# A hybrid decoder layer on one core: x transposed before it is normalised, the norm factors applied behind the first projection, last products and results tile by tile

## The reference

```
h  = RMSNorm(x) * g1
q_a,k_a,v_a | q_b,k_b,v_b | gate_a | gate_b = split(h @ W_in)      # 1024 x 4352
x += (sigmoid(gate_a) * (A @ W_a) + sigmoid(gate_b) * (B @ W_b)) @ W_o   # A, B: two attentions
x += CrossAttn(RMSNorm(x), RMSNorm(mem))                           # 256 memory tokens
x += HierMoE(RMSNorm(x))       # top-1 of 4 groups, top-2 of 8 experts, 32 gated MLPs of 256
out = RMSNorm(x) * g_final
RMSNorm(x) = x * (mean(x*x) + 1e-6) ** -0.5, row by row
```

## Time and profile before

| | us |
|---|---|
| median of 3 runs (lowest, highest) | 463.2 (462.82, 464.59) |
| the profiled execution's own time | 462.48 |
| its span, first to last instruction | 460.7 |
| PE busy | 405.1 |
| DVE busy | 176.8 |
| ACT busy | 166.3 |
| POOL busy | 38.9 |

### The profile page before, as it was taken

The page is one execution under the profiler, slowest core; times in us unless marked ns, Lnnn a source line. Parts: engine busy times, 40 slices in busy tenths (PEclk is TensorE's granted clock), DMA queues, the critical chain, the costliest instruction groups (busy, mean ns, idle before and its releaser), DMA issues.

```text
span 460.7 us, 7793 instructions
## 1 busy us (share of the span) xinstructions
PE 405.1 (88%) x3113; PEld 302.7 (66%) x3113; DVE 176.8 (38%) x314; ACT 166.3 (36%) x320; POOL 38.9 (8%) x81
## 2 busy tenths in 40 slices
PE   3999999999999999999999898989895758768476
PEld 3999998999999999999895343434251322413223
DVE  3663754766458846546444111111201101002003
ACT  6744657576468544567535000000100001001004
POOL 4010242223000000000302000000000000000000
PEclk9999999999999999999998999999999988979979
DMA  8878874767745855558989999999999999999992
GB/s 297 219 203 271 269 246 157 229 198 232 256 138 175 282 185 183 177 166 285 363 265 358 345 413 410 409 410 406 409 410 410 409 410 409 410 410 410 410 379 91
DMA packets 66228, 139.53 MB, mean 303 GB/s; under 512 B 6646, under 2 KB 40470, under 8 KB 66198
## 3 DMA queue, kind: packets, MB, share of 16 engines
q1 hardware_dynamic: 66192, 139.12, 82.7%
q10 hardware_dynamic: 6, 0.00, 0.0%
HBM read 138.06 MB, written 1.05 MB: 302 GB/s over the span
## 4 chain that ended last, share of the span: by engine, by line
PE 71%; DMA 11%; SPq 10%; DVE 2%; ACT 2%; issue 2%; POOLq 0%; POOL 0%; DVEq 0%; ACTq 0%
PE proj L1186 13%; PE proj L1187 13%; PE proj L1188 13%; DMA moe_slot<-in_expert_w_up_dram 10%; PE proj L1431 9%; SPq L365 5%; PE score L1455 4%; PE score L1405 3%; SPq L370 3%; SPq L364 3%; PE attno L1463 2%; PE attno L1261 1%; PE probt L1187 1%; PE probt L1188 1%; PE probt L1186 1%
## 5 line engine op out<-in xcount | busy, mean ns | idle before, releaser
L823 DVE TENSOR_TENSOR w_lo<-w_raw,w_hi 128x1024 fp32r<-128x1024 f32 x66 | 81.2, 1231 | 45.0 <-ACT w_hi L568 44.6
L1431 PE MATMUL proj<-moe_slot,moe_x 128*32 128x512 f32 x512 | 66.8, 668 | 30.2 <-DMA moe_slot<-in_expert_w_up_dram 22.5
L568 ACT ACTIVATE w_hi<-w_raw 128x1024 fp32r<-128x1024 f32 x66 | 69.8, 1059 | 30.5 <-PE proj L1188 21.8
L1186 PE MATMUL proj<-hT_hi,w_hi 128*128 128x256 f32 x232 | 67.2, 290 | 0.0
L1187 PE MATMUL proj<-hT_lo,w_hi 128*128 128x256 f32 x232 | 65.6, 283 | 0.0
L1188 PE MATMUL proj<-hT_hi,w_lo 128*128 128x256 f32 x232 | 65.6, 283 | 0.0
L1431 PEld LDWEIGHTS proj<-moe_slot,moe_x 128*32 128x32 f32 x512 | 17.7, 120 | 67.6 <-issue 56.1
L777 ACT ACTIVATE silu_g<-proj 128x256 f32<-128x256 f32 x8 | 3.1, 383 | 152.1 <-PE proj L1431 152.1
L1186 PEld LDWEIGHTS proj<-hT_hi,w_hi 128*128 128x128 f32 x232 | 44.4, 191 | 3.2 <-issue 2.0
L1187 PEld LDWEIGHTS proj<-hT_lo,w_hi 128*128 128x128 f32 x232 | 44.4, 192 | 0.0
L1188 PEld LDWEIGHTS proj<-hT_hi,w_lo 128*128 128x128 f32 x232 | 44.4, 191 | 0.0
(11 more groups left out here) (266 smaller groups left out, 755.1 us busy)
## 6 DMA issues: line engine op xcount, KB each, us to landing
moe_slot<-in_expert_w_gate_dram SPq DMA_DIRECT2D x64, 512.0 KB, 14.6
moe_slot<-in_expert_w_up_dram SPq DMA_DIRECT2D x64, 512.0 KB, 15.2
moe_slot<-in_expert_w_down_dram SPq DMA_DIRECT2D x64, 512.0 KB, 14.7
w_raw<-in_w_in_dram SPq DMA_DIRECT2D x34, 512.0 KB, 4.4
w_raw<-in_xattn_wkv_dram SPq DMA_DIRECT2D x8, 512.0 KB, 3.5
w_raw<-in_mix_out_w_dram SPq DMA_DIRECT2D x8, 512.0 KB, 3.5
w_raw<-in_moba_out_w_dram SPq DMA_DIRECT2D x4, 512.0 KB, 3.9
w_raw<-in_swa_out_w_dram SPq DMA_DIRECT2D x4, 512.0 KB, 3.5
```

What stands on the lines that cost most here:

```text
L568: act.activation(w_hi[:, g % NS], w_raw[:, g % NW], ACT.Copy).then_inc(hi_done, 1)
L823: dve.tensor_tensor(w_lo[:, g % NS], w_raw[:, g % NW], w_hi[:, g % NS].bitcast(F32), ALU.subtract)\
L1186: pe.matmul(ps, a[0], b[0], start=start, stop=False, skip_group_check=True)
L1431: op = pe.matmul(PJ[0][e * WIN:(e + 1) * WIN, :].rearrange("p (j f) -> p j f", j=2), moe_x[:, k, e * WIN:(e + 1) * WIN], both_w[:, r], sta ...
```

## The change

- The tiles of x are transposed as they land. Their squares are still summed and the factors still computed, but no engine needs them before a result of the first projection is copied out.
- The copies of chunks 0 to 16 multiply by the factors. For qa, ka, qb, kvb and the gates the token runs along the free axis, so the factors are needed as a row on all partitions (`rnorm_row`): PE makes it by two products, DVE copies it. These copies move from ACT to DVE. For va the token is the partition; ACT keeps that copy, now one for each tile.
- SP's queue begins with the first norm's weights, then tile 0, weight half 0, tile 1, halves 1 and 2. The other three norm weights are loaded from ACT's queue.
- The small products for sinks and biases, and the transpose of the three other norm weights, move behind the third weight half (g == 2), together with the two products for `rnorm_row`.
- At the end products and squares go tile by tile, POOL adds epsilon itself, and ACT issues one of the four stores.

```diff
-    ON_DVE = {"merge": 1, "mix": 1, "xo": 2}
+    ON_DVE = {"qa": 1, "ka": 1, "qb": 1, "kvb": 1, "gate": 1, "merge": 1, "mix": 1, "xo": 2}
@@ SP
-            for t in range(TT):
-                sp.dma_start(xres[:, t], x[0, t * P:(t + 1) * P, :]).then_inc(x_in[t], 16)
-            for i, g in enumerate((mix_norm_g, mem_norm_g, xattn_norm_g, ffn_norm_g)):
-                sp.dma_start(g_rows[i * KD:(i + 1) * KD, :], g[0].rearrange("(k p) -> k p", p=P)).then_inc(gain_in, 16)
-            for g in range(NW):
+            sp.dma_start(g_first[:], mix_norm_g[0].rearrange("(k p) -> k p", p=P)).then_inc(first_gain_in, 16)
+            sp.dma_start(xres[:, 0], x[0, 0:P, :]).then_inc(x_in[0], 16)
+            load_half(0)
+            sp.dma_start(xres[:, 1], x[0, P:T, :]).then_inc(x_in[1], 16)
+            for g in range(1, NW):
                 load_half(g)
...
-            for t in range(TT):
-                for half, scaled in ((1, fin_dve), (0, fin_act)):
-                    cols = slice(half * 512, (half + 1) * 512)
-                    sp.wait_ge(scaled, t + 1)
-                    sp.dma_start(out[0, t * P:(t + 1) * P, cols], fin_rows[:, t, cols]).then_inc(out_done, 16)
+            for t, half in ((0, 1), (0, 0), (1, 1)):
+                cols = slice(half * 512, (half + 1) * 512)
+                sp.wait_ge(fin_dve if half else fin_act, t + 1)
+                sp.dma_start(out[0, t * P:(t + 1) * P, cols], fin_rows[:, t, cols]).then_inc(out_done, 16)
@@ POOL
-            inverse_root(4)
+            for t in range(TT):
+                pool.wait_ge(sq_done, sq_count(FINAL_NORM, t))
+                pool.tensor_scalar(mean_eps[:, FINAL_NORM, t:t + 1], mean_sq[:, FINAL_NORM, t, 0:1],
+                                   mean_sq[:, FINAL_NORM, t, 1:2], EPS, ALU.add, ALU.add).then_inc(ms_done, 1)
+                pool.wait_ge(ms_done, 2 * FINAL_NORM + t + 1)
+                pool.tensor_tensor(rnorm[:, FINAL_NORM, t:t + 1], mean_eps[:, FINAL_NORM, t:t + 1], mhalf[:, 0:1],
+                                   ALU.pow).then_inc(rs_done, 1)
@@ ACT
+            for i, g in enumerate((mem_norm_g, xattn_norm_g, ffn_norm_g)):
+                act.dma_start(g_rows[i * KD:(i + 1) * KD, :], g[0].rearrange("(k p) -> k p", p=P)).then_inc(gain_in, 16)
...
-            for t in range(TT):
-                act.wait_ge(x_in[t], 16)
-                whole_squares(0, xres, t)
-            act.wait_ge(rs_done, 1)
-            act.activation(xn[:, 0], xres[:, 0], ACT.Copy, scale=rnorm[:, 0, 0:1]).then_inc(x0n_done, 1)
+            act.wait_ge(x_in[0], 16)
+            whole_squares(0, xres, 0)
             split_hi(0)
...
             unit_hi(0, hT_hi, 3)
+            act.wait_ge(x_in[1], 16)
+            whole_squares(0, xres, 1)
             for c in range(FIRST_UNDER):
                 split_hi(2 * c + 2)
                 split_hi(2 * c + 3)
-                evacuate(c)
+                if kinds[c] not in ON_DVE:
+                    evacuate(c)
...
+            act.wait_ge(fin_act, TT)
+            act.dma_start(out[0, P:T, 0:512], fin_rows[:, 1, 0:512]).then_inc(out_done, 16)
@@ DVE
+            def evacuate(c):
+                k, i, src = kinds[c], kinds[:c].count(kinds[c]), PJ[c % 2]
+                two = src[:].rearrange("p (a n) -> p a n", a=2)
+                rows = rnorm_row[:].unsqueeze(1).broadcast_to([P, 2, T])
+                dve.wait_ge(half_done, 2 * c + 2)
+                if k in ("qa", "qb"):
+                    op = dve.scalar_tensor_tensor(out=(qa if k == "qa" else qb)[:, 2 * i:2 * i + 2], in0=two,
+                                                  scalar=float(HD) ** -0.5, in1=rows, op0=ALU.mult, op1=ALU.mult)
...
+                else:
+                    op = dve.tensor_tensor(gates[:, 2 * i:2 * i + 2], two, rows, ALU.mult)
+                op.then_inc(ev_dve, 1)
...
-            normalise(0, xres, [1])
...
+            for t in range(TT):
+                means(0, t)
             for c in range(FIRST_UNDER):
                 split_lo(2 * c + 2)
                 split_lo(2 * c + 3)
+                if c == 0:
+                    dve.wait_ge(row_ps, 1)
+                    dve.tensor_copy(rnorm_row[:], PO[1][:, T:2 * T]).then_inc(row_set, 1)
...
+                    dve.wait_ge(row_set, 1)
+                if kinds[c] in ON_DVE:
+                    evacuate(c)
                 if c == 1:
                     normalise(MEM_NORM, mem_raw)
...
                 split_lo(2 * c + 3)
+                evacuate(c)
                 if 2 <= i <= UNITS + 1:
                     mix_out_lo(i - 2)
@@ PE
-            pe.transpose(PO[0][:, 0:4 * KD], g_rows[:], ident[0:4 * KD, 0:4 * KD]).then_inc(c_gain_ps, 1)
-            transpose_normalised(((x0n_done, 1), (xn_done, 1)))
+            pe.transpose(PO[0][:, 0:KD], g_first[:], ident[0:KD, 0:KD]).then_inc(c_gain_ps, 1)
+            for t in range(TT):
+                pe.wait_ge(x_in[t], 16)
+                for u in range(4):
+                    op = transpose_unit(NT_BANKS, xres, u, t)
+                    if t == TT - 1:
+                        op.then_inc(nt_ps, 1)
...
+                if g == 2:
+                    consts = PO[0][:, P:]
...
+                    pe.wait_ge(rs_done, TT)
+                    for t in range(TT):
+                        op = pe.matmul(PO[1][:, T + t * P:T + (t + 1) * P],
+                                       rnorm[:, 0, t:t + 1].broadcast_to([P, P]), ident[:], start=True, stop=True)
+                    op.then_inc(row_ps, 1)
...
                     back_to_tokens(0, 0)
-                    back_to_tokens(1, 0)
                     pe.wait_ge(y_dve, n + 1)
-                    for t in range(TT):
-                        back_to_tokens(t, 1)
+                    back_to_tokens(0, 1)
+                    for half in range(2):
+                        back_to_tokens(1, half)
```

More of the change, by code:

```diff
@@ L480, in _ @@
             inverse_root(0)
[L481 removed]
+            pool.wait_ge(c_gain, 2)
             pool.wait_ge(wr_in, 32)
@@ L663, in _ @@
             split_hi(2 * at["merge"] + 2)
-            act.wait_ge(ev_act, evac_count(last["gate"]))
+            act.wait_ge(ev_dve, evac_count(last["gate"]))
             sigmoids(0)
@@ L866, in mix_out_lo @@
                     .then_inc(mix_lo, 1)
-            normalise(0, xres, [1])
+            def evacuate(c):
[6 more added lines that the diff above has]
+                                                  scalar=float(HD) ** -0.5, in1=rows, op0=ALU.mult, op1=ALU.mult)
+                elif k == "ka":
+                    op = dve.tensor_tensor(ka[:, 2 * i:2 * i + 2], two, rows, ALU.mult)
+                elif k == "kvb":
+                    for g in range(2):
+                        for half in range(2):
+                            dve.tensor_tensor(kb2[half * HD:(half + 1) * HD, g], src[g * HD:(g + 1) * HD, 0:T],
+                                              rnorm_row[g * HD:(g + 1) * HD], ALU.mult)
+                    for t in range(TT):
+                        op = dve.tensor_scalar(vb[:, t], src[:, T + t * P:T + (t + 1) * P], rnorm[:, 0, t:t + 1], None,
+                                               ALU.mult)
+                else:
+                    op = dve.tensor_tensor(gates[:, 2 * i:2 * i + 2], two, rows, ALU.mult)
+                op.then_inc(ev_dve, 1)
             dve.wait_ge(c_gain_ps, 1)
-            dve.tensor_copy(gains[:], PO[0][:, 0:4 * KD].rearrange("p (n k) -> p n k", n=4)).then_inc(c_gain, 1)
+            dve.tensor_copy(gains[:, 0], PO[0][:, 0:KD]).then_inc(c_gain, 1)
             split_lo(0)
@@ L1226, in pair_scores @@
                 swa, i = divmod(j, PAIRS)
-                pe.wait_ge(ev_act, evac_count(at["kvb"] if swa else at["ka"] + i // 2))
+                pe.wait_ge(ev_dve, evac_count(at["kvb"] if swa else at["ka"] + i // 2))
                 if j:
@@ L1252, in pair_values @@
                 swa, i = divmod(j, PAIRS)
-                pe.wait_ge(ev_act, evac_count(at["kvb"] if swa else at["va"] + i // 2))
+                if swa:
+                    pe.wait_ge(ev_dve, evac_count(at["kvb"]))
+                else:
+                    pe.wait_ge(ev_act, evac_count(at["va"] + i // 2))
                 pe.wait_ge(pt_sb, 2 * j + 2)
@@ L1279, in _ @@
                     half_chunk(g, hT_hi, hT_lo)
-            pe.wait_ge(c_gain, 3)
+                if g == 2:
+                    consts = PO[0][:, P:]
+                    pe.wait_ge(c_gain, 1)
+                    pe.wait_ge(gain_in, 48)
+                    pe.transpose(consts[:, 0:3 * KD], g_rows[:], ident[0:3 * KD, 0:3 * KD])
+                    consts = consts[:, 3 * KD:]
+                    pe.wait_ge(c_ones, 1)
+                    pe.wait_ge(small_in, 48)
+                    pe.matmul(consts[:, 0:HEADS], ones[0:1, :], sink_row[:], start=True, stop=True)
+                    pe.matmul(consts[:, HEADS:HEADS + NG + NE], ones[0:1, :], br[:], start=True, stop=True)
+                    pe.wait_ge(rs_done, TT)
```

(5 more changed lines are left out.)

92 lines of the change are left out of this document (38 added, 54 removed).

## The result

The changed kernel took 466.2 us (median of 20 runs, 464.6 to 467.6) against 463.3 for the kernel before on the same chip: a ratio of 1.0056, with a 95% interval from 1.004 to 1.0073. The ratios of this document compare means, so they are not the quotients of the medians beside them, and two executions of the kernel before, of 1022 and 2219 us, are left out of this one. Forecast were 462.8 us and a range up to 464.8, so both the time and the sign of the change were missed. The profiled execution of the changed kernel took 464.86 us of its own, with a span of 463.0; the kernel before, 462.48 and 460.7. These 2.4 us can be followed through the two traces. In the table a row is a place in the program, in us from the start of the span; the first four are starts in PE's timelines.

A forecast was written before the change was run, and what follows sets the result against it. PE's pace was taken to bound the kernel until 133 us and the start of the later expert-load stream; -1.8 + 0.75 + 0.15 + 1.5 - 0.45 = +0.15 on 462.48 gave 462.6, forecast 462.8 us, range 460.9 to 464.8 (8 in 10).

The forecast's parts named there:

- tile 1 at 7.4: At the start, tile 1 of x lands at 7.4 us behind weight half 0; bounds 6.7 and 8.5.
- the clock term: At the start, TensorE's clock rises late because PE's transposes are broken up by gaps: +1.5 us, bounds 0 and 2.5.
- the step from the profile to the median: Sum on the profiled execution gave 462.6; only part of its 0.7 below the median was added, giving 462.8 us.
- First product, -1.8: At the start, PE's first projection product comes at 9.9 instead of 11.7 us: -1.8, bounds -2.5 and -0.7.
- The cross-check in the prediction: At the start, the queue carries the same bytes up to tile 1 as it did before up to 7.36 us.
- lands at 8.5, first product at 11: Rival at the start: tile 1 lands late behind a weight half, clock as late, 463.9 us; chance 0.15.
- Constants, +0.75: Between weight halves 2 and 3, PE does small products, norm-weight transpose and `rnorm_row` products: +0.75 us, bounds 0.5 and 1.1.
- DVE behind `rnorm_row`, +0.15: At `w_lo` of half 4, DVE's way of 2.9 us stalls PE: +0.15 us, bounds 0 and 1.2.
- The rival of a DVE stall of 1.5 us: Rival around `rnorm_row`: DVE's way takes 4 us, costing 1.5 in all, 464.3 us; chance 0.13.
- Copies on DVE, 0: In projections and attention, copies moved from ACT to DVE cost nothing, up to +1 if one delays a `w_lo`.
- The end, -0.45: At the end, the last two stores go out together and the last lands near 459.9: -0.45 us, bounds -0.9 and 0.
- the 0.05 above 465.5: Chance of a measurably slower kernel, above 465.5 us: late landing of tile 1 and DVE's stall together, 0.05.

The follow-up runs named there:

- e14: e10 with the first norm's weights issued behind tile 1 of x instead of first; 465.3 us, ratio 1.004.
- e13: e10 with weight half 1 and all loads behind it held until tile 0 has landed; 462.5 us, ratio 0.9968.
- e1: Changed kernel with PE's gaps before the first product filled by identity transposes that nobody reads (12, 9 and 5); 462.5 us, ratio 0.999.
- e8: The changed kernel run once more, unaltered; 465.9 us, ratio 1.0044.
- e2: Changed kernel with tile 1 of x loaded ahead of weight half 0; 466.5 us, ratio 1.0073.
- e5: e1 with the norm-weight transpose and the products for sinks and biases moved between the two tiles; 462.4 us, ratio 0.9977.
- e7: Kernel before with 28 filling transposes at the start and the changed kernel's new end; 461.4 us, ratio 0.9963.
- e3: Kernel before with 28 filling identity transposes ahead of its first transpose; 461.6 us, ratio 0.9967.
- `A`: The changed kernel, against the kernel before; 466.2 us, ratio 1.0056.
- `B`: The kernel before the change, base of the ratios; 463.3 us.
- e11: e7 with the experts' norm weights and both router-weight loads issued behind weight half 3; 461.15 us, ratio 0.9954.
- e12: Changed kernel with only the 12 filling transposes at the start, none behind the tiles; 465.7 us, ratio 1.0052.
- e9: The kernel before once more, unaltered, for its trace; profiled own time 462.34 us.
- e4: Kernel before with only the changed kernel's new end; 463.8 us, ratio 1.0001.
- e6: e1 with the three other norm weights loaded from SP's queue behind weight half 2, not ACT's; 462.3 us, ratio 0.998.
- e10: e5 with the experts' norm weights and both router-weight loads issued behind weight half 3; 462.3 us, ratio 0.998.

## Why the prediction was wrong

Against the profile's own times the forecast sum was +0.15 and the traces say +2.4. Three steps failed: "tile 1 at 7.4", the size of the clock term, and the step from the profile to the median. By the terms:

- **First product, -1.8: was -0.5.** The step that failed is "tile 1 at 7.4". It landed at 8.4 in the profile, and between 8.38 and 8.79 in the five profiles with the same loads. The cross-check in the prediction (the queue carries the same bytes up to 7.36 as before) left out its own first line, the 0.45 us of the issue ahead (e14: 0.5 on tile 0, 0.34 on tile 1), and took transfers to be served one behind the other; when the two halves right behind it were held back, tile 1 landed 0.5 us earlier (e13). The remaining 0.3 are hops: from the landing to the first product it took 2.8 us, not 2.5. The rival "lands at 8.5, first product at 11" was this, at 0.15.
- **The clock, +1.5: was +2.5** (e1). The mechanism was right, a rise of the clock that comes only behind the first product. Its size was not: I let the 3.5 us that the rise had taken in the earlier trace rows stand for the rise behind the first product, and it took 5.5. One execution can't give that number: it was 5.2 in e8 and 4.7 in e2, and behind work from 1.58 on between under 3 (e1) and 6 us (e5). The bound of 2.5 held.
- **Constants, +0.75: were 1.27 in the chain.** The two `rnorm_row` products were put at 0.45 and took 0.64; the transpose of 24 rows, 0.17; sinks and biases 0.46 where 0.15 to 0.55 was said, and I had taken the low end. With DVE's part the stretch grew by 1.24, against 0.90 forecast. e5 shows that 0.8 of it need not have been on PE's path.
- **DVE behind `rnorm_row`, +0.15: was 0.04.** The way was 2.5 us, not 2.9. The rival of a DVE stall of 1.5 us was false; between the two `w_lo` stand six instructions, where it counted nine.
- **Copies on DVE, 0: right.** From the first step to the router's logits both traces take the same 193.0 us.
- **The end, -0.45: was -0.63** in the table, and with fillers -0.5 from the last landing on (e7 against e3).
- **From the profile to the median.** Here the forecast added 0.2 us, since the clock term was "already that of an average start". `A`'s median lies 1.3 above its profile; `B`'s lies 0.8 above, between its two groups. The spread of the three times shown before (462.82 to 464.59) was a hint that one kernel has two starts, and I read it as noise.

Of the 3.4 us that were missed (462.8 against 466.2), some 2.2 lie in the terms: 1.3 for tile 1, 1.0 for the clock, 0.3 for constants and DVE, less 0.4 to 0.5 for the end and the stretch between router and experts. The other 1.1 lie in the step to the median. What came true is the rival of a late tile together with the clock term at its bound of 2.5. With its own bounds the prediction would have had -0.7 + 0.75 + 0.15 + 2.5 - 0.45 = +2.25, close to the +2.4 of the traces. But the rival of the late tile kept the clock at 1.5 (463.9), and the 0.05 above 465.5 was given to a late tile with a DVE stall; late tile and later clock together had no chance of their own. Whether a longer gap also makes the clock later is not shown: in e2 tile 1 came at 5.87, and the products were slow for 4.7 us all the same.

## What to carry to other kernels

Work taken off the chain at the start is only worth what lands in its place: look up which transfer is now the last to arrive, and count the issues ahead of it and the transfers read beside it. Work that kept PE warm has a value that no chain shows; before breaking it up, ask what PE does in the new gaps, and fill them with products that nobody reads (`A` is 0.56% slower, e1 no different from `B`; e11 is 0.46% faster, together with the end). They cost nothing only while PE waits: in e14 nine of them stood in the chain with 1.55 us. Then compare filled with filled, for a change can look neutral only because the kernel that it is measured against pays for something else in half of its executions. When the times of a kernel fall into two groups, one profile shows one of them: look at the list of times before taking a median as a base.

## What was not expected of the hardware

- The clock fell within a gap of 2.96 us after it had risen (e12), and rose again only 3.6 us into steady products; gaps of 2.27 us (e1) and 1.90 (e3) left it up.
- The time of the first rise varied: with PE at work from 1.58 on it was there by 4.5 (e1), at 4.9 (e12) and near 7.6 (e5). In `A` and e8, with pieces of work before, it came 5.5 and 5.2 us into the products, in e2, with one piece of 3.7 us before, 4.7. Whether pieces delay it was not separated.
- A load of 4 KB issued behind three of 512 KB landed 4.9 us after its issue (e14); the same load issued first had landed by 2.7.
- The issue of one load of 128 KB in short rows held SP for 4.56 us in `A`, 2.1 in the profile of before, and 1.6 in e11.

Still open: between 242 and 256 us ten of the sixteen profiles (`B`, e9, e4, e11, e12, e2, e5, e6, e13, e14) show PE at half clock for 3.4 us, and six (`A`, e8, e1, e3, e7, e10) do not. The windows of `B` and `A`:

```profile
239.30:249.20 9.90, 9.50 (x54) 6.73 (x53) 5.97 (x36) 7.36 (x15) 1.06 (x2) 0.83 0.95 371
242.60:252.00 9.40, 7.61 (x52) 5.76 (x51) 5.77 (x34) 7.37 (x15) 1.08 (x2) 1.00 0.93 352
```

It lies in the stretch in which the table has -0.28, and is the only difference seen there. What decides whether and where it comes, and whether it is behind the 1.7 to 3.2 us by which the runs of one filled kernel still spread, or behind the 2.5 us in the stage of the experts (e14), was not settled. Nor was the rest of tile 1's delay: e13 and e14 together would account for 0.9 of 1.0 us, and were not tried together.
